# Two transfers in place of one for the spare experts' weights in a two-block transformer kernel

## The reference, cut to what matters

```python
def hier_moe(h, wgc, bgc, wgf, bgf, w1, w3, w2):
    t = h.reshape(B * S, D)
    pg = jax.nn.softmax(t @ wgc + bgc, axis=-1)
    gw, gi = lax.top_k(pg, 1)
    ...
    tv, ti = lax.top_k(jax.nn.softmax(fs, axis=-1), TOP_K_IN_GROUP)
    eid = gi * EXPERTS_PER_GROUP + ti
    gates = jnp.sum(jax.nn.one_hot(eid, N_EXPERTS) * (gw * tv)[..., None], axis=1)
    a = jnp.einsum('td,edf->tef', t, w1)
    c = jnp.einsum('td,edf->tef', t, w3)
    act = jax.nn.silu(a) * c * gates[:, :, None]
    y = jnp.einsum('tef,efd->td', act, w2)
```

## Time and profile before

| | us |
|---|---|
| median of 3 runs | 3187.71 |
| lowest and highest of them | 3180.34, 3190.59 |
| profiled execution | 3186.9 |
| its span, first to last instruction | 3184.8 |

### The profile page before, as it was taken

How to read it: one execution, slowest core, us unless ns; L and a number is a source line. 1 busy time by engine, 2 the same in 40 slices (tenths; PEclk the granted TensorE clock), 3 DMA queues, 4 the chain that set the end, 5 groups by cost and what they waited for, 6 DMA issues and landing times. The chain is left out here.

```text
span 3184.8 us, 36203 instructions
## 1 busy us (share of the span) xinstructions
PE 2898.0 (91%) x12892; PEld 2265.0 (71%) x12892; DVE 1702.7 (53%) x2406; ACT 1063.8 (33%) x1845; POOL 1518.7 (48%) x920
## 2 busy tenths in 40 slices
PE   7989999999999899999999599898978798899976
PEld 5778777888877688778888467676745566676754
DVE  4865554442158655544421664646744565647744
ACT  2533323221035333322210414334533315235533
POOL 4543356666755333566667353663212245652231
PEclk9999999999999899999999799899989899989988
DMA  4211122323322111223332121146940321238912
GB/s 138 75 62 58 50 79 80 98 93 99 94 85 73 60 54 53 73 82 96 99 93 93 66 77 49 60 174 231 355 179 9 129 66 41 80 150 305 342 57 80
DMA packets 84729, 337.22 MB, mean 106 GB/s; under 512 B 18288, under 2 KB 21104, under 8 KB 76016
## 3 DMA queue, kind: packets, MB, share of 16 engines
q1 hardware_dynamic: 67600, 302.80, 28.1%
q0 software_dynamic: 15264, 26.26, 2.3%
q10 hardware_dynamic: 1728, 6.29, 0.5%
HBM read 370.93 MB, written 30.41 MB: 126 GB/s over the span
## 5 line engine op out<-in xcount | busy, mean ns | idle before, releaser
L179 POOL TENSOR_SCALAR wh<-ring 128x1024 fp32r<-128x1024 f32 x348 | 379.6, 1091 | 1101.8 <-PE ps L244 929.9
L181 POOL TENSOR_TENSOR wl<-ring,wh 128x1024 fp32r<-128x1024 f32 x348 | 848.1, 2437 | 29.0
L242 PE MATMUL ps<-xh,wh 128*128 128x512 f32 x1760 | 720.4, 409 | 69.0 <-PEq L680 22.8
L243 PE MATMUL ps<-xl,wh 128*128 128x512 f32 x1760 | 697.9, 397 | 0.0
L244 PE MATMUL ps<-xh,wl 128*128 128x512 f32 x1760 | 697.3, 396 | 0.0
L242 PEld LDWEIGHTS ps<-xh,wh 128*128 128x128 f32 x1760 | 339.0, 193 | 162.7 <-issue 57.3
L243 PEld LDWEIGHTS ps<-xl,wh 128*128 128x128 f32 x1760 | 338.9, 193 | 75.1 <-issue 6.3
L244 PEld LDWEIGHTS ps<-xh,wl 128*128 128x128 f32 x1760 | 337.9, 192 | 73.3
L1328 DVE SCALAR_TENSOR_TENSOR taps<-ps,par,taps 128x511 f32<-128x511 f32 x192 | 143.9, 749 | 249.9 <-ACT taps L1095 234.6
L2618 DVE TENSOR_TENSOR ew_l<-ew,ew_h 128x1024 fp32r<-128x1024 f32 x184 | 218.3, 1242 | 71.0 <-ACT ew_h L2220 70.5
L2031 PE MATMUL ps<-ew,hactT 128*128 128x512 f32 x368 | 187.2, 656 | 61.7 <-DVE hactT L2631 61.7
(11 more groups left out here) (443 smaller groups left out, 5104.5 us busy)
## 6 DMA issues: line engine op xcount, KB each, us to landing
ring<-in_w SPq DMA_DIRECT2D x348, 512.0 KB, 3.5
ew<-in_ew SPq DMA_DIRECT2D x32, 2048.0 KB, 9.3
ew<-in_ew SPq DMA_DIRECT2D x32, 1024.0 KB, 9.2
yg<-ypicks SPq DMA_DIRECT2D x16, 512.0 KB, 6.6
xrows<-xr ACTq DMA_DIRECT2D x8, 512.0 KB, 2.6
z<-in_x SPq DMA_DIRECT2D x4, 512.0 KB, 8.5
gw<-in_gw SPq DMA_DIRECT2D x2, 1024.0 KB, 6.9
out<-z SPq DMA_DIRECT2D x8, 256.0 KB, 2.9
```

The lines of the kernel that those rows point to most:

```text
L179: nc.gpsimd.tensor_scalar(hi, raw, 1.0, 0.0, ALU.mult, ALU.add).then_inc(sem["w_hi"], 1)
L181: nc.gpsimd.tensor_tensor(lo, raw, hi, ALU.subtract).then_inc(sem["w_split"], 1)
L242: nc.tensor.matmul(out, wh, xh, start=first, stop=False, **kw)
L243: nc.tensor.matmul(out, wh, xl, start=False, stop=False, **kw)
```

## The change

The expert weights stand in DRAM as two tensors, in_eu (rows of 4096) and in_ed (rows of 2048), where in_ew had rows of 6144. SP's loads take from these, in the same order as before. load_spare is replaced by spare_up and spare_down, two indirect DMAs with waits and semaphores of their own (`es_up0`, `es_up1`, `es_dn0`, `es_dn1`). spare_up for tile j + 3 stands at the head of GpSimd's turn j and waits for expert_up(j); spare_down for tile j + 2 stands where load_spare stood. ScalarE waits for the first, TensorE's expert_down for the second. From the third spare tile on each also waits until the transfer two before it, on the same semaphore, has landed.

```diff
-                    def load_spare(j):
-
-                        b, k, last = j % EW_BUFS, j - EXPERTS, (layer + 1) * ROWS_E - 1
-                        nc.gpsimd.indirect_dma_start(ew[:, b, :], None, d_ew, bass.IndirectOffsetOnAxis(ap=spare[:, k:k + 1], axis=0),
-                                                     bounds_check=last, oob_is_err=False).then_inc(sem[f"ew_sp{b}"], 16)
+                    def spare_up(j):
+
+                        k, last = j - EXPERTS, (layer + 1) * ROWS_E - 1
+                        g.wait_ge(sem["up_mm"], at("up_mm", UP_PARTS * (j - EW_BUFS + 1)))
+                        if k >= 2:
+                            g.wait_ge(sem[f"es_up{k % 2}"], at(f"es_up{k % 2}", 16 * (k // 2)))
+                        nc.gpsimd.indirect_dma_start(ew[:, j % EW_BUFS, 0:EW_UP], None, d_eu[:, :],
+                                                     bass.IndirectOffsetOnAxis(ap=spare[:, k:k + 1], axis=0),
+                                                     bounds_check=last, oob_is_err=False).then_inc(sem[f"es_up{k % 2}"], 16)
+
+                    def spare_down(j):
+
+                        k, last = j - EXPERTS, (layer + 1) * ROWS_E - 1
+                        g.wait_ge(sem["dn_mm"], at("dn_mm", j - EW_BUFS + 1))
+                        if k >= 2:
+                            g.wait_ge(sem[f"es_dn{k % 2}"], at(f"es_dn{k % 2}", 16 * (k // 2)))
+                        nc.gpsimd.indirect_dma_start(ew[:, j % EW_BUFS, EW_UP:], None, d_ed[:, :],
...
                     for j in range(TILES):
+                        if EXPERTS <= j + EW_BUFS < TILES:
+                            spare_up(j + EW_BUFS)
                         if j + 3 < TILES:
                             gather_rows(j + 3)
-                        if EXPERTS <= j + 2 < TILES:
-                            g.wait_ge(sem["dn_mm"], at("dn_mm", j))
-                            load_spare(j + 2)
+                        if EXPERTS <= j + EW_BUFS - 1 < TILES:
+                            spare_down(j + EW_BUFS - 1)
                         if j:
                             scatter_rows(j - 1)
...
@@ expert_down, TensorE
-                            pe.wait_ge(sem[f"ew_sp{b}"], at(f"ew_sp{b}", 16 * ((j - EXPERTS) // EW_BUFS + 1)))
+                            k = j - EXPERTS
+                            pe.wait_ge(sem[f"es_dn{k % 2}"], at(f"es_dn{k % 2}", 16 * (k // 2 + 1)))
@@ weights_high, ScalarE
-                            act.wait_ge(sem[f"ew_sp{b}"], at(f"ew_sp{b}", 16 * ((j - EXPERTS) // EW_BUFS + 1)))
+                            k = j - EXPERTS
+                            act.wait_ge(sem[f"es_up{k % 2}"], at(f"es_up{k % 2}", 16 * (k // 2 + 1)))
@@ load_up, load_down, SP
-                        sp.dma_start(ew[:, b, 0:EW_UP], d_ew[row:row + P, 0:EW_UP]).then_inc(sem[f"ew_up{b}"], 16)
+                        sp.dma_start(ew[:, b, 0:EW_UP], d_eu[row:row + P, :]).then_inc(sem[f"ew_up{b}"], 16)
-                        sp.dma_start(ew[:, b, EW_UP:], d_ew[row:row + P, EW_UP:]).then_inc(sem[f"ew_dn{b}"], 16)
+                        sp.dma_start(ew[:, b, EW_UP:], d_ed[row:row + P, :]).then_inc(sem[f"ew_dn{b}"], 16)
```

More of the change, by code:

```diff
@@ L1409, with second_block @@
         **{f"ew_{w}{n}": 16 * turns_of(EXPERTS, n, EW_BUFS) for w in ("up", "dn") for n in range(EW_BUFS)},
-        **{f"ew_sp{n}": 16 * (turns_of(TILES, n, EW_BUFS) - turns_of(EXPERTS, n, EW_BUFS)) for n in range(EW_BUFS)},
+        **{f"es_{w}{n}": 16 * turns_of(TILES - EXPERTS, n, 2) for w in ("up", "dn") for n in range(2)},
         **{f"yg_in{c}": 32 for c in range(4)}}
-def second_block(nc, mem, sh, d_cst, d_tab, d_w, first_unit, d_par, d_p, d_rt, d_ew, xrows, ypicks, out):
+def second_block(nc, mem, sh, d_cst, d_tab, d_w, first_unit, d_par, d_p, d_rt, d_eu, d_ed, xrows, ypicks, out):
     with ExitStack() as ctx:
@@ L1500, in second_block @@
                  "rt_in", "xrow_mm", "xrow_evac", "xrow_out", "xg_in0", "xg_in1", "xgt_mm", "xgt_lo", "xgt_hi",
-                 "ew_up0", "ew_up1", "ew_up2", "ew_dn0", "ew_dn1", "ew_dn2", "ew_sp0", "ew_sp1", "ew_sp2", "e_hi", "e_lo", "up_mm", "silu", "hact", "hactt_mm", "hactt",
+                 "ew_up0", "ew_up1", "ew_up2", "ew_dn0", "ew_dn1", "ew_dn2", "es_up0", "es_up1", "es_dn0", "es_dn1", "e_hi", "e_lo", "up_mm", "silu", "hact", "hactt_mm", "hactt",
                  "dn_half", "dn_mm", "y_lo", "y_hi", "y_out0", "y_out1", "yg_in0", "yg_in1", "yg_in2", "yg_in3", "zt_mm", "zt_taken",
@@ L1663, in gather_rows @@
                                                      bounds_check=S - 1, oob_is_err=False).then_inc(sem[f"xg_in{j % 2}"], 16)
-                    def load_spare(j):
-                        b, k, last = j % EW_BUFS, j - EXPERTS, (layer + 1) * ROWS_E - 1
-                        nc.gpsimd.indirect_dma_start(ew[:, b, :], None, d_ew, bass.IndirectOffsetOnAxis(ap=spare[:, k:k + 1], axis=0),
-                                                     bounds_check=last, oob_is_err=False).then_inc(sem[f"ew_sp{b}"], 16)
+                    def spare_up(j):
[12 more added lines that the diff above has]
+                        nc.gpsimd.indirect_dma_start(ew[:, j % EW_BUFS, EW_UP:], None, d_ed[:, :],
+                                                     bass.IndirectOffsetOnAxis(ap=spare[:, k:k + 1], axis=0),
+                                                     bounds_check=last, oob_is_err=False).then_inc(sem[f"es_dn{k % 2}"], 16)
                     def scatter_rows(j):
@@ L1695, in _ @@
                     g.wait_ge(sem[f"y_out{n}"], DEPTH * PER2[f"y_out{n}"])
-                for b in range(EW_BUFS):
-                    g.wait_ge(sem[f"ew_sp{b}"], DEPTH * PER2[f"ew_sp{b}"])
+                    g.wait_ge(sem[f"es_up{n}"], DEPTH * PER2[f"es_up{n}"])
+                    g.wait_ge(sem[f"es_dn{n}"], DEPTH * PER2[f"es_dn{n}"])
                 nc.gpsimd.dma_reset(sem_range)
@@ L2707, in build @@
         ypicks = nc.dram_tensor("ypicks", (PICKS, D), F32, kind="Internal").ap()
-        second_block(nc, mem, sh, d["cst2"], d["tab"], d["w"], DEPTH * U1, d["par2"], d["p"], d["rt"], d["ew"], xrows, ypicks, out)
+        second_block(nc, mem, sh, d["cst2"], d["tab"], d["w"], DEPTH * U1, d["par2"], d["p"], d["rt"], d["eu"], d["ed"], xrows, ypicks, out)
 def _blocks(w):
@@ L2845, in _second_layout @@
     out["cst2"] = np.concatenate([cst[n] for n in CST2], 1).astype(np.float32)
-    w2, par, experts = [], [], []
+    w2, par, expert_up, expert_down = [], [], [], []
     for l in range(DEPTH):
@@ L2859, in _second_layout @@
         down = a["moe_w2_2"][l].reshape(EXPERTS, EC, P, D).transpose(0, 2, 1, 3)
-        experts.append(np.concatenate([up.reshape(ROWS_E, EW_UP), down.reshape(ROWS_E, EW_DOWN)], -1))
+        expert_up.append(up.reshape(ROWS_E, EW_UP))
+        expert_down.append(down.reshape(ROWS_E, EW_DOWN))
         lam0 = 0.8 - 0.6 * np.exp(-0.3 * l)
@@ L2887, in _second_layout @@
     out["w"] = w2
-    out["ew"] = np.concatenate(experts, 0)
+    out["eu"], out["ed"] = np.concatenate(expert_up, 0), np.concatenate(expert_down, 0)
     tok = np.arange(P, dtype=np.float32)[:, None]
```

## The result

The changed kernel takes 3105.78 us, the median of 4 runs (3097.22 to 3109.34), against 3187.14 us for the kernel before in the same comparison. The ratio is 0.9743, with a 95% interval of 0.9716 to 0.9771: 2.6% faster, 82 us with 73 to 91 as its interval. The prediction was 3106 us. The profiled execution has a span of 3100.8 us, 84.0 less than before.

A forecast was written before the change was run, and what follows sets the result against it. TensorE bounds the kernel, losing time only in the spare-tile stretches through idling and its lower clock. Gains of 46.65 us (layer 0) and 34.64 us (layer 1), together 81.3, from 3186.9 give 3105.6, forecast 3106 us, range 3098 to 3111.

The forecast's parts named there:

- the ruler: VectorE's copies of y's second half, one per tile: regular tiles 10.02 us apart, forecast for all 23 tiles.
- my bounds of 7.8 and 12.3: Tile 16's 2 MB up load on the software queue: lands 7.8 to 12.3 us after issue, at 2330.1 to 2334.6.
- The limit: Tile 16's up load may land until 2336.4 without costing TensorE, allowing VectorE's 0.48 us idle; 1.8 us of margin.
- Parts taken as zero: Down load, seven more GpSimd issues per layer, waits on transfer k - 2, and regular loads from contiguous tensors: no cost.
- A: Added GpSimd issues hold VectorE, 0.42 to 0.9 us in each of fourteen tiles: 3112 to 3119 us; chance 0.08.
- its own sign: On VectorE: runs of four ew_l pieces lasting more than 4.62 us would show that added issues hold it.
- One row of the forecast: GpSimd's 1.99 us gather inside three ew_l pieces lasting an unchanged 3.50 us, read as VectorE losing nothing.
- the lock in the Trainium skill: VectorE and GpSimd's shared port locked for a whole instruction, the other fully blocking; VectorE's half left out of the sum.
- B: Tile 16 late or software queue slow beside SP's: three real tiles 2 to 4 us over, 3112 to 3118; chance 0.08.
- C: Empty tiles keep their gaps; only the three long periods shrink, to 13.6 us: 31.1 us gained, 3156 us; chance 0.03.
- D: Up issue reaches the queue no earlier, GpSimd being stuck in the turn before: 3188 to 3200 us; chance 0.02.
- E: Contiguous layout slows SP's regular loads, each us beyond the free 0.6 costing 26 us; 50% slower gives 3213; chance 0.03.

The follow-up runs named there:

- experiment 1: Changed kernel with both spare transfers issued where the single load stood, up first: 3179.41 us, ratio 0.9984 against the kernel before.
- experiment 2: Changed kernel with only the up loads of spare tiles 16 and 17 early, those of 18 to 22 at the old place: 3141.16 us, ratio 0.9862.
- 5: Changed kernel with the gather issued ahead of the up load, which starts 2.4 us later for tile 16: 3104.75 us, ratio 0.9752.
- 6: Changed kernel with the up load behind the down load, 4.5 us later for tile 16 and 6.7 for the others: 3111.2 us, ratio 0.9766.
- the probes: Changed kernel, SP waiting for each spare up load, then copying 16 KB to show its landing: 3102.85 and 3099.31 us, one execution each.
- experiment 3: Changed kernel with SP's loads of experts 0 to 15 read from the old tensor with rows of 6144: 3100.96 us, ratio 0.9734.
- 4: Changed kernel without spare loads on GpSimd; SP loads all 23 tiles, experts 0 to 6 in tiles 16 to 22: 3103.1 us, ratio 0.9731.

## Why the prediction was right

**The bound and the ruler.** TensorE's idle time, and its matmuls at the lower clock, were the whole of it. Layer 0's stage, from the first copy of y to the last, shrank from 262.19 to 215.52 us, layer 1's from 250.15 to 215.53: 46.67 and 34.62, together 81.29 us against 81.3 forecast. The other 2.7 us of the span lie where the change does nothing: the work between the two layers' stages took 433.9 us before and 430.2 after, and 429.0 to 437.2 in the other kernels here, and the first stage began 1.3 us later. They are spread between executions, and a part of the good agreement of 3105.78 with 3106 is luck of that size.

**The cause of the waits.** That the landing of the up weights sets the gaps, for owned and empty tiles alike, is shown from three sides: with the load at the old place the gaps stay (experiment 1), moved for some tiles they go for those (2), and moved back in steps a delay returns only in tiles whose load is late (5, 6).

**Landing in time.** The issue came where forecast: 0.8 us behind the up matmuls, 14.5 us ahead of the down load (14.6 forecast). The landing at 9.9 to 11.4 us, by the probes, lies between my bounds of 7.8 and 12.3, which were not safe ones: the same load behind the gather took up to 13.7. The limit was too strict by 1.0 us. ScalarE wants the data 13.6 us behind the issue (2336.14 + 1.05 against 2323.60) and may have it 1.48 us later, so 15.1 us against a landing of 11.4: 3.7 us of room where I had 1.8. The two errors work in opposite directions.

**Parts taken as zero.** The down load, the added issues and the layout cost nothing that can be measured (experiments 3 and 4, both with every period at 10.02 us).

**The rivals.** A, that VectorE is held by the added issues, falls by its own sign: the runs of four pieces last 4.62 us with 1.93 and 2.00 us of issues inside them. One row of the forecast was read too strongly: the gather at 2392.38 starts inside the last of three ew_l pieces and runs on for 0.9 us past their end at 2393.47, so their unchanged 3.50 us could not have shown a loss, and the runs of four can. Of the lock in the Trainium skill, "SBUF — State Buffer", who interferes with whom, this trace shows again only GpSimd waiting for a piece of VectorE; the other half is not seen for descriptor writing here. That section of the Trainium skill ties the contention of a VectorE instruction with two SBUF inputs, as ew_l's are, to a GpSimd instruction that reads SBUF, a condition that the forecast left out. Whether the issue of an indirect DMA meets it, no run here shows. B, tile 16 late, did not happen in the changed kernel, but does in five of six layers when the gather goes first, at 0.6 to 1.0 us each. C is wrong by the seven periods of 10.02 us in each layer and by experiment 2, D by the rows of GpSimd. E, the slower layout, is wrong by experiment 3.

## What to carry to other kernels

Where a buffer has parts that come free at different times, give each part its own transfer and its own wait; the split alone brought 5 us here, the earlier wait the other 77. A load that moves nothing still has its round trip (3.0 us here), and an engine that waits for it pays: eleven such loads cost 3.6 us of period each on average, 1.1 us of it through the lower clock. Put the load that somebody will wait for ahead of small transfers in the same queue, where their waits can't hold it, and before trusting a margin find the whole distance to the engine that sets the end, not only the first idle row.

## What the runs showed of the hardware

Behind a gather of 128 rows of 4 KB in the software queue, issued 1.3 us earlier, a 2 MB load landed 13.3 to 13.7 us behind its issue in five of six cases, and 9.9 to 11.4 us in the other order, beside SP's loads (DMA share from issue to landing 0.72 to 0.85 in the five, 0.89 to 0.94 in the other order). The exchange so moved the landing by some 3 us more than the 2.4 us by which it moved the issue; which of the two, the gather or the later start, does it, is not shown.

A gap of the same 2.25 us on TensorE has two prices. Timeline of TensorE with the split alone, layer 0:

```profile
2403.36 5.40 PE L2047 MATMUL ps<-ew,hactT 128*128 128x512 f32 x8 [2.26 <-DVE hactT L2648]
2417.59 3.70 PE L2047 MATMUL ps<-ew,hactT 128*128 128x512 f32 x8 [2.25 <-DVE hactT L2648]
```

The granted clock of the two groups, by stretch, columns as above:

```profile
2403.36:2408.76 5.40, 5.40 (x9) 2.38 (x10) 1.53 (x3) 1.54 (x2) 0.50 (x1) 0.68 0.01 0
2417.59:2421.29 3.70, 3.70 (x9) 1.79 (x10) 1.52 (x3) 1.54 (x2) 0.51 (x1) 1.00 0.04 5
```

The eight down matmuls behind the gap take 5.40 us at a mean granted clock of 0.68, so partly at the lower level, or 3.70 us at 1.00, and this is the whole difference between the empty tiles' periods of 14.2 and 12.5 us. Seven of the eleven empty tiles paid it in the kernel before; what decides between the two is not shown.
